# A two-layer hybrid decoder step on one core: a later wait in the FFNs, one activation table for the norms' roots, another order at two places of the mixing, and an end that goes bank by bank

## What is computed

```
x = x + 0.5 * SwiGLU_1(RMSNorm(x))
h = RMSNorm(x); P = h @ w_in                # RWKV7 | RG-LRU | GatedDeltaNet | GLA columns
o = concat[RWKV7(P_rw), RGLRU(P_rg), GatedDeltaNet(P_gdn), GLA(P_gla)]
x = x + o @ w_out
x = x + 0.5 * SwiGLU_2(RMSNorm(x))
```

```
def _rmsnorm(x, w):
    y = x * lax.rsqrt(jnp.mean(x * x, axis=-1, keepdims=True) + NORM_EPS)
    return y * w
def _swiglu(x, w_gate, w_up, w_down):
    return (jax.nn.silu(x @ w_gate) * (x @ w_up)) @ w_down
```

## Time and profile before

| | |
|---|---|
| Median of 3 runs (least, most) | 1389.3 us (1388.21, 1390.75) |
| The profiled execution's own time | 1388.47 us |
| Its span in the trace | 1386.7 us |
| Busy: PE, DVE, ACT, POOL | 98%, 62%, 50%, 5% |
| DMA: moved, mean rate | 185.85 MB, 134 GB/s |

### The profile page before, as it was taken

The page is one execution under the profiler, slowest core; times in us unless marked ns, Lnnn a source line. Parts: engine busy times, 40 slices in busy tenths (PEclk is TensorE's granted clock), DMA queues, the critical chain, the costliest instruction groups (busy, mean ns, idle before and its releaser), DMA issues. The chain is left out here.

```text
span 1386.7 us, 31381 instructions
## 1 busy us (share of the span) xinstructions
PE 1353.0 (98%) x12556; PEld 1308.9 (94%) x12556; DVE 862.9 (62%) x1329; ACT 691.4 (50%) x970; POOL 75.4 (5%) x109
## 2 busy tenths in 40 slices
PE   7999999999999999999999999999999999999997
PEld 7999999988888999999999999998888899999997
DVE  6656533897777765553475565358977767566433
ACT  7454433846455745443374453347455556454422
POOL 0000000200030100000010000010001301000000
PEclk9999999999999999999999999999999999999999
DMA  8544444313212544444454444433232135444441
GB/s 297 167 151 149 146 144 151 117 55 106 78 49 92 187 161 151 151 151 141 149 188 146 151 150 152 151 122 107 78 95 77 63 129 165 149 151 148 148 148 48
DMA packets 50765, 185.85 MB, mean 134 GB/s; under 512 B 5760, under 2 KB 6272, under 8 KB 50176
## 3 DMA queue, kind: packets, MB, share of 16 engines
q1 hardware_dynamic: 49104, 177.37, 39.4%
q10 hardware_dynamic: 1584, 7.35, 1.5%
HBM read 180.14 MB, written 4.56 MB: 133 GB/s over the span
## 5 line engine op out<-in xcount | busy, mean ns | idle before, releaser
L477 PE MATMUL ps<-xh,wh 128*128 128x320 f32 x1952 | 613.7, 314 | 12.7 <-DVE xl L1523 7.4
L1501 DVE TENSOR_TENSOR wl<-raw,wh 128x1024 fp32r<-128x1024 f32 x332 | 407.0, 1227 | 337.6 <-ACT wh L1124 337.2
L479 PE MATMUL ps<-xh,wl 128*128 128x320 f32 x1952 | 604.2, 310 | 0.0
L478 PE MATMUL ps<-xl,wh 128*128 128x320 f32 x1952 | 604.1, 310 | 0.0
L1124 ACT ACTIVATE wh<-raw 128x1024 fp32r<-128x1024 f32 x332 | 348.6, 1053 | 382.5 <-PE ps L479 371.5
L477 PEld LDWEIGHTS ps<-xh,wh 128*128 128x128 f32 x1952 | 367.5, 188 | 24.5 <-DVE wl L1501 7.8
L478 PEld LDWEIGHTS ps<-xl,wh 128*128 128x128 f32 x1952 | 367.7, 188 | 0.8
L479 PEld LDWEIGHTS ps<-xh,wl 128*128 128x128 f32 x1952 | 367.5, 188 | 0.0
L477 PE MATMUL ps<-hid_h,wh 128*128 (+1 forms) x704 | 217.9, 310 | 2.1 <-DVE hid_l L1548 2.1
L479 PE MATMUL ps<-hid_h,wl 128*128 (+1 forms) x704 | 217.5, 309 | 0.0
L478 PE MATMUL ps<-hid_l,wh 128*128 (+1 forms) x704 | 217.5, 309 | 0.0
(11 more groups left out here) (293 smaller groups left out, 974.5 us busy)
## 6 DMA issues: line engine op xcount, KB each, us to landing
raw<-wts SPq DMA_DIRECT2D x332, 512.0 KB, 3.5
ms<-mst ACTq DMA_DIRECT2D x2, 1440.0 KB, 9.2
mout<-ms ACTq DMA_DIRECT2D x2, 1440.0 KB, 7.2
x<-xT SPq DMA_DIRECT2D x4, 320.0 KB, 5.3
yT<-x SPq DMA_DIRECT2D x4, 320.0 KB, 2.2
cs<-cst SPq DMA_DIRECT2D x1, 652.0 KB, 9.0
pr<-par ACTq DMA_DIRECT2D x1, 429.0 KB, 4.1
pr<-par ACTq DMA_DIRECT2D x1, 425.0 KB, 5.2
```

What stands on the lines that cost most here:

```text
L477: pe.matmul(out, a, rh, start=start, stop=False)
L478: pe.matmul(out, a, rl, start=False, stop=False)
L479: return pe.matmul(out, b, rh, start=False, stop=stop)
L1501: tt(wl[:, s, :], raw_of(layer, n), wh[:, s, :].bitcast(F32), ALU.subtract).then_inc(lo_ready.sem, 1)
```

## The change

**FFN.** PE waits for hidden tile FT-2 instead of FT-3 before `down(0)`, and for all 22 only before unit 20. The loop over down units has four turns instead of five; units 17 to 21 are written out behind it.

**Roots.** ACT loads the table set that holds both ln and exp (`natural_log_exp_and_others`) ahead of `norm_split` for the two norms that follow an FFN, after the first split in layer 0, and, for the norm behind the mixing, where it had loaded `natural_log`. The load in `rms` goes, and the one that the compiler put before exp.

**Mixing opening.** On DVE `evac(5)` stands directly behind `rw_decay`, both ahead of the low splits `ahead(4)` and `ahead(5)`, and `evac(7)` ahead of `rw_scaled`. On ACT `ahead(5)` follows `ahead(4)`.

**Inverse's second level.** On DVE `gdn_conv(2)` goes from before `evac(12)` to behind `rw_gain`, which now follows the inverse at once, and `ahead(12)` behind the convolution.

**End.** The last two down units go bank by bank together, six products (0.88 us) a bank. POOL adds the squares of tiles 0 to 3 to that of tile 7 in a chain of four, PE makes four sums. ACT loads its table ahead of the squares, scales x[0] and x[1] by their weights, and writes the root twice, first to PSUM bank 0, then to SBUF. DVE scales six tiles by the root in PSUM, POOL the two others by the one in SBUF. The transfers go in the order 1, 2, 0, 3.

```diff
@@ PE, ffn
-                on(pe, layer, hl_ready, f * FT + FT - 3)
+                on(pe, layer, hl_ready, f * FT + FT - 2)
...
+                def last_two():
+                    order = bank_order(layer, f)
+                    pe.wait_ge(lo_ready.sem, layer * UNITS + base + FFN_UNITS)
+                    for m in order:
+                        for k in (FT - 2, FT - 1):
+                            ins = three(ps[:, m, 0:TOK], *wsl(slot(layer, base + 2 * FT + k), m), hid_h[:, k, :], hid_l[:, k, :],
+                                        False, k == FT - 1)
...
                 down(0, start=True)
-                on(pe, layer, hl_ready, (f + 1) * FT)
-                with pe.Fori(0, (FT - 2) // RING) as i:
+                with pe.Fori(0, (FT - 5) // RING) as i:
                     for k in range(1, 1 + RING):
                         down(k, i)
-                down(FT - 1, stop=True)
+                for k in range(1 + (FT - 5) // RING * RING, FT - 2):
+                    down(k)
+                on(pe, layer, hl_ready, (f + 1) * FT)
+                if (layer, f) == (DEPTH - 1, 1):
+                    last_two()
+                else:
+                    down(FT - 2)
+                    down(FT - 1, stop=True)
@@ PE, end
-            pe.wait_ge(pair_sq.sem, 1)
+            pe.wait_ge(g_step.sem, G_ALL + 4)
             final_sum(7, start=True)
-            for k in (3, 4, 5):
+            for k in (4, 5, 6):
                 pe.wait_ge(sq_ready.sem, DEPTH * 24 + k + 2)
...
@@ ACT
             def norm_split(layer, which, name):
+                if which < 2:
+                    act.preload_act_table_set("natural_log_exp_and_others")
...
                 split_hi(layer, LAST_UNIT[which] + 1)
-                act.preload_act_table_set("natural_log")
                 act.wait_ge(sum_mm.sem, layer * 3 + which + 1)
...
-                ahead(4)
+                ahead(4, 5)
                 act.preload_act_table_set("natural_log_exp_and_others")
...
-                ahead(5)
...
+            act.preload_act_table_set("natural_log_exp_and_others")
             for n, k in enumerate((KT - 1, *range(KT - 1))):
...
+                if k in (0, 1):
+                    act.wait_ge(sq_ready.sem, DEPTH * 24 + n + 1)
+                    act.activation(x[:, k, :], x[:, k, :], ACT.Copy, scale=C("nf", k, 1)).then_inc(a_step.sem, 1)
...
+            act.activation(ps[:, 0, 0:TOK], lnt[:], ACT.Exp, scale=-0.5).then_inc(rstd_ready.sem, 1)
             act.activation(rstd[:], lnt[:], ACT.Exp, scale=-0.5).then_inc(rstd_ready.sem, 1)
@@ DVE
                 evac(4)
-                ahead(4)
                 rw_decay()
                 evac(5)
+                ahead(4)
                 ahead(5)
                 rw_mix(0, 2)
                 evac(6)
                 rw_keys()
+                evac(7)
                 rw_scaled()
-                evac(7)
...
                 ahead(11)
-                gdn_conv(2)
                 evac(12)
                 inverse(0, 1)
+                rw_gain()
+                gdn_conv(2)
                 ahead(12)
-                rw_gain()
...
-            for k in range(KT):
-                stt(x[:, k, :], x[:, k, :], C("nf", k, 1), rstd[:], ALU.mult, ALU.mult).then_inc(x_new.sem, 1)
+            for k in range(2, KT):
+                stt(x[:, k, :], x[:, k, :], C("nf", k, 1), ps[:, 0, 0:TOK], ALU.mult, ALU.mult).then_inc(x_new.sem, 1)
@@ POOL, end
-            for a, b, n in ((7, 0, 2), (1, 2, 4)):
-                apart(gp, sq_ready, DEPTH * 24 + n)
-                gp.tensor_tensor(nsq[:, a, :], nsq[:, a, :], nsq[:, b, :], ALU.add).then_inc(pair_sq.sem, 1)
+            for k in range(4):
+                apart(gp, sq_ready, DEPTH * 24 + k + 2)
+                if k:
+                    apart(gp, g_step, G_ALL + k)
+                gp.tensor_tensor(nsq[:, 7, :], nsq[:, 7, :], nsq[:, k, :], ALU.add).then_inc(g_step.sem, 1)
+            apart(gp, a_step, DEPTH * A_STEPS + 2)
+            apart(gp, rstd_ready, DEPTH * 3 + 2)
+            for k in range(2):
+                gp.tensor_tensor(x[:, k, :], x[:, k, :], rstd[:], ALU.mult).then_inc(g_step.sem, 1)
```

More of the change, by code:

```diff
@@ L128 @@
 V_STEPS, A_STEPS, G_STEPS = 102, 40, 14 + 3 * 6
+G_ALL = DEPTH * G_STEPS - 6
 class Signal:
@@ L375, in program @@
         out_read = signal("out_read", KT - 1)
-        bank_done, pair_sq = signal("bank_done", 2 * (KT - 1)), signal("pair_sq", 2)
+        bank_done = signal("bank_done", 2 * (KT - 1))
         gs_ready, gu_read, sil_ready, act_ready, hh_ready, hl_ready = (
@@ L461, in _ @@
             stream(done, DEPTH * UNITS)
-            for s in range(4):
-                sp.wait_ge(x_new.sem, DEPTH * 24 + 2 * s + 2)
+            for s, done, n in ((1, x_new, DEPTH * 24 + 2), (2, x_new, DEPTH * 24 + 4), (0, g_step, G_ALL + 6), (3, x_new, DEPTH * 24 + 6)):
+                sp.wait_ge(done.sem, n)
                 sp.dma_start(yT[:, 2 * s:2 * s + 2, :], x[:, 2 * s:2 * s + 2, :]).then_inc(y_out.sem, 16)
@@ L584, in down @@
                     ins.then_inc(unit_used.sem, 1)
+                def last_two():
[5 more added lines that the diff above has]
+                                        False, k == FT - 1)
+                            if m == order[-1]:
+                                ins.then_inc(unit_used.sem, 1)
+                        if m != order[-1]:
+                            ins.then_inc(bank_done.sem, 1)
                 down(0, start=True)
-                on(pe, layer, hl_ready, (f + 1) * FT)
-                with pe.Fori(0, (FT - 2) // RING) as i:
+                with pe.Fori(0, (FT - 5) // RING) as i:
                     for k in range(1, 1 + RING):
                         down(k, i)
-                down(FT - 1, stop=True)
+                for k in range(1 + (FT - 5) // RING * RING, FT - 2):
[6 more added lines that the diff above has]
+                    down(FT - 1, stop=True)
             def each(fn, chunks=range(NC)):
@@ L1104, in final_sum @@
                 return pe.matmul(ps[:, 7, 0:TOK], C("ones"), nsq[:, k, :], start=start, stop=stop)
-            pe.wait_ge(pair_sq.sem, 1)
+            pe.wait_ge(g_step.sem, G_ALL + 4)
             final_sum(7, start=True)
-            for k in (3, 4, 5):
+            for k in (4, 5, 6):
                 pe.wait_ge(sq_ready.sem, DEPTH * 24 + k + 2)
[L1110 to L1114, removed]
+                ins = final_sum(k, stop=k == 6)
+            ins.then_inc(sum_mm.sem, 1)
         @block.scalar
@@ L1484, in _ @@
                 act.activation(nsq[:, k, :], x[:, k, :], ACT.Square).then_inc(sq_ready.sem, 1)
-            act.preload_act_table_set("natural_log_exp_and_others")
+                if k in (0, 1):
+                    act.wait_ge(sq_ready.sem, DEPTH * 24 + n + 1)
+                    act.activation(x[:, k, :], x[:, k, :], ACT.Copy, scale=C("nf", k, 1)).then_inc(a_step.sem, 1)
             act.wait_ge(sum_mm.sem, DEPTH * 3 + 1)
             act.activation(lnt[:], ps[:, 7, 0:TOK], ACT.Ln, bias=C("e6"), scale=1.0 / D).then_inc(a_step.sem, 1)
-            act.wait_ge(a_step.sem, DEPTH * A_STEPS + 1)
+            act.wait_ge(a_step.sem, DEPTH * A_STEPS + 3)
+            act.activation(ps[:, 0, 0:TOK], lnt[:], ACT.Exp, scale=-0.5).then_inc(rstd_ready.sem, 1)
             act.activation(rstd[:], lnt[:], ACT.Exp, scale=-0.5).then_inc(rstd_ready.sem, 1)
@@ L2275, in _ @@
                 apart(gp, state_out, layer * 32 + 32)
-            for a, b, n in ((7, 0, 2), (1, 2, 4)):
-                apart(gp, sq_ready, DEPTH * 24 + n)
-                gp.tensor_tensor(nsq[:, a, :], nsq[:, a, :], nsq[:, b, :], ALU.add).then_inc(pair_sq.sem, 1)
+            for k in range(4):
[7 more added lines that the diff above has]
+                gp.tensor_tensor(x[:, k, :], x[:, k, :], rstd[:], ALU.mult).then_inc(g_step.sem, 1)
+        assert g_step.given == G_ALL
         for s in [a_step, in_read] + [s.whole if isinstance(s, Stage) else s for s in S.values()]:
```

## The result

The changed kernel takes 1381.7 us (median of 5 runs, 1379.6 to 1384.6). The kernel before took 1388.2, 1389.3, 1389.9 and 1390.8 us beside it, and 4643.9 in a fifth run, which is left out here; what disturbed that one is not known. The ratio is 0.9945 with a 95% interval of 0.9934 to 0.9956: faster by 0.55%, some 7.6 us, where 1381.0 and a range of 1375.5 to 1385.0 had been forecast. The profiled execution took 1379.63 for 1388.47 before, and its span is 1377.8 us for 1386.7, that is 8.9 us less. The sum had said 8.3.

The account below looks back on a forecast made before the run. PE, busy 98% of the span, was taken as the bound. Terms 3.14 + 2.14 + 3.2 + 0.2 - 1.4 + 1.05 = 8.3 us took 1388.47 to 1380.15, plus 0.8 for the median: 1381.0 (80% range 1375.5 to 1385.0).

Parts of the forecast that it names:

- FFN, the hidden wait: Before `down(0)`: PE's wait for the late hidden part goes, 2.1 idle + 4 x 0.26 = 3.14 us saved.
- Roots: Four FFN loops: waits for `gus` behind `rstd` go, since ACT loses at least one 1.28 us load; 2.14 us saved.
- Mixing opening: Earlier root and DVE's new order bring the end of `rw_rest` forward: 1.6 us per layer, 3.2 in two.
- tile 7 ends on PE only at 277.22 + 0.31: Mixing opening: tile 7 ends at 277.53, so DVE waits for PE before `evac(7)`, some 1.3 us of new idle time.
- Rival 3: Mixing opening gives nothing: ACT, held at `ahead(5)`, brings `rw_scaled` its exponentials late; 1384.4 us, chance 0.08.
- Second level: Inverse: PE's gain is given back at the third level, reached at DVE's pace; 0, plus 0.2 of layer 0's lateness.
- Rival 1: DVE isn't the pace between opening and third level, so second-level waits are gained: about 5.5 us more, 1375.5, chance 0.10.
- The load ahead of the norms' splits: Three norms: the load makes `xh` late and `xl` late by 0.4 to 0.5; 3 x 0.47 = 1.4 us lost.
- PE starts the next tiles on it: Norm passes: PE starts its next tiles on `xl`, so `xl`'s lateness of 0.4 to 0.5 us delays PE.
- Rivals 2 and 4: Norms: DVE's `xl` beside POOL's adds, 1383.4, chance 0.15; table switches hold ACT longer than their load, 1384.9, chance 0.03.
- The end: Final sums, scalings and transfers: 0.5 us from fewer sums, 0.55 from scaling and transfers, together 1.05 saved.
- Rival 5: Slower: PE's waits gather at the third level and the half-speed clock returns after them and the opening; 1390, chance 0.02.

Follow-up runs that it names:

- the part alone: The kernel before with only the FFN's hidden wait moved (changed down loop, without the bank-by-bank end): 1387.0 us, ratio 0.9986.
- the one with the hidden load: The changed kernel with the norms' table load ahead of each FFN's last weight split, in ACT's idle time: 1379.8 us, ratio 0.9935.
- With 288 products fewer: The changed kernel with the down loop kept at five turns in three of the four FFNs: 1379.2 us, ratio 0.9931.
- the last run: The changed kernel with hidden load, `evac(7)` behind `rw_scaled`, five-turn loop and `ahead(14)` behind `gdn_bounds`: 1375.7 us, ratio 0.9905 to the kernel before.
- the split behind `gdn_bounds`: The changed kernel with `ahead(14)` behind both the last convolution and `gdn_bounds` on DVE: 1378.9 us, ratio 0.9929.

## Why the prediction was right, point by point

- **FFN, the hidden wait** (-3.14): -3.12, four steps as idle time plus 0.26 gave them. Shown, by the change's own trace and by the part alone (3.13). What the sum left out is that the written-out units make PE's program longer (4 units of 24 products in each of four FFNs, 384 products), which came with 1.2 us lost in layer 1's recurrences; no term was taken for it.
- **Roots** (-2.14): -2.22, and the 1.28 us load was more than enough.
- **Mixing opening** (-1.6 a layer): -2.06 and -2.06. The mechanism held, the size was short. DVE did wait before `evac(7)`, 1.05 us for the 1.3 forecast. The mis-sized step was "tile 7 ends on PE only at 277.22 + 0.31": PE had two small waits ahead of it, for DVE's inputs of the gates (L612, 263.29) and for `evac(5)` (273.74), and these went too (0.22 and 0.14 in layer 0), so tile 7 ended earlier itself. Rival 3 (ACT late at `ahead(5)`) didn't come.
- **Second level** (0, with 0.2): 0.2 less in layer 0, 0.15 more in layer 1. That DVE sets the pace was argued from its 33.6 busy microseconds of 35; the run with its old order (no change in time) and the one with 0.84 us of added work (0.86 and 0.85 later) show it. Rival 1 is refuted. One thing was placed wrong: the prediction looked for all that is given back at L792, the third level's second product (333.70). But 1.90 of the 3.36 us in layer 0, and 1.90 of 1.99 in layer 1, came at the same level's first product, L774 at 327.20, where PE hadn't waited at all. So its sign, the wait at L792 grown in both layers to 2 us or more, did not come: the wait is 1.39 in both, and in layer 1 it had been 1.30. By the prediction's own words that would have spoken for rival 1; the time did not, since DVE's order ends there too (`inverse(0, 2)`).
- **The load ahead of the norms' splits** (+1.4): +0.91. `xl` was late by about 0.5 as forecast, but PE lost 0.24, 0.25 and 0.42. The step that failed is "PE starts the next tiles on it", as if PE had been waiting when `xl` came: it was ready at 243.02, 0.35 before PE began at 243.37, where in the changed kernel PE begins 0.15 behind it (241.78, 241.93). So 0.2 of the lateness cost nothing, and in two norms the shorter pass gave 0.18 back. Rivals 2 and 4 didn't come: the pass got shorter, not longer, behind its start (0.54 for the 0.90 us of the second `xl`), and the load starts 0.02 us after the split, `xh` 0.01 after the load. The Trainium skill's 1380 ns of drain for each switch (ScalarE: Activation LUTs, What ACT_TABLE_LOAD costs) does not show there.
- **The end** (-1.05): -1.0, with errors of both signs in its parts. POOL's chain has steps of 1.06, not 1.15, and held PE up by 0.2 us in place of 0.5, so the sums gave 0.8 for 0.5; the scaling and the transfers gave 0.2 for 0.55.
- **Rival 5** (slow clock): not in this execution. But three variants of the changed kernel fell into half speed right behind the third level's wait of 1.8 us, as the rival says, so the executions without a trace, three of them with lower clocks, may have done so; that is not shown.

That the total was right to 0.6 us in the profiled execution was luck in part, because errors of both signs met: start, opening and norms together 1.9 better, PE's new idle time 1.2 worse. That the median came within 0.7 of 1381.0 rests on the same, and on four slower executions of which no trace is kept.

## What to carry to other kernels

Where two engines are both nearly full, a wait seen on one is not yet a gain: look for the next wait behind which the other engine's queue ends, and take its busy time between the two places. What fills a hole is decided by the engine that arrives last, so an order that removes PE's wait by making DVE wait (here `evac(7)`) can cost more than it gives. A table load, or anything else that waits for no data, belongs into idle time that is already there, even one instruction away from where it seems to belong. And written-out code may not be free on an engine that is never idle: it moved the places at which PE waits for its code.

## What the runs showed of the hardware that had not been expected

- PE idled for 0.2 to 1.1 us with nothing to wait for among short matmuls (0.01 to 0.1 us apart) of the recurrences. In all nine programs with the unrolled down units it is at the same matmul of layer 1, 0.7 to 1.1 us in eight of them, 0.4 in the one with the hidden load. With 288 products fewer it is 0.3, further on; in the last run, which has the same PE code, there are three, of 0.6, 0.2 and 0.3. All 22 such idle times end 1.3 to 1.6 us after a 16 KB packet of the instruction queue is through; that queue has 63 packets in the nine programs, 61 in these two and 60 in the kernel before. What decides which packet is late stays open.
- The granted clock fell to half, 1.2 GHz for 2.4, for 3.4 us behind PE's waits in the inverse, in one layer, both or none of an execution of one kernel or another. Each of the ten cost PE 1.5 to 1.7 us. In all but one program (the split behind `gdn_bounds`) PE's next waits, at L812 above all, took most of it up again; an eleventh in a recurrence (layer 0, with `evac(7)` moved back) cost 1.5, found no such wait and stayed. The trace of the hidden wait alone shows that it had cost the kernel before nothing: layer 0's stretch is missing there, PE comes to L792 (L795 there) 1.5 us sooner, and waits 1.30 for ACT where it hadn't.
